# Sparse attention scores from split queries and keys, with mask and distance added on VectorE

## What is computed

```python
sc = jnp.einsum('bqgrd,bcgd->bgrqc', qb, ck).astype(f32) * scale           # compressed
sc = jnp.where(ok_c, sc - slopes[:, :, None, None] * dist_c, NEG_INF)
...
ss = jnp.where(dist_s[:, :, None] >= 0,                                     # selected
               ss - slopes[None, :, :, None, None, None] * dist_s[:, :, None], NEG_INF)
...
sw = jnp.einsum('bqgrd,bkgd->bgrqk', qb, kwb).astype(f32) * scale          # window
sw = jnp.where(ok_w, sw - slopes[:, :, None, None] * dist_w.astype(f32), NEG_INF)
p_win = jax.nn.softmax(sw, axis=-1)
...
o = gb[..., 0:1] * o_cmp + gb[..., 1:2] * o_slc + gb[..., 2:3] * o_win
```

## Time and profile before

| | |
|---|---|
| median of 3 runs | 3684.37 us (3681.41 to 3687.91) |
| span of the profiled execution | 3682.4 us |
| TensorE busy | 3545.7 us (96%) |
| VectorE busy | 1694.4 us (46%) |
| ScalarE busy | 1230.5 us (33%) |
| GpSimd busy | 204.2 us (6%) |
| `sparse_attention` | 1142.2 to 1323.3, 181.1 us |
| `compressed_and_keys` | 999.6 to 1142.2, 142.6 us |

### The profile page before, as it was taken

The page is one execution under the profiler, slowest core; times in us unless marked ns, Lnnn a source line. Parts: engine busy times, 40 slices in busy tenths (PEclk is TensorE's granted clock), DMA queues, the critical chain, the costliest instruction groups (busy, mean ns, idle before and its releaser), DMA issues. The chain is left out here.

```text
span 3682.4 us, 45186 instructions
## 1 busy us (share of the span) xinstructions
PE 3545.7 (96%) x18232; PEld 2772.9 (75%) x18232; DVE 1694.4 (46%) x2770; ACT 1230.5 (33%) x2143; POOL 204.2 (6%) x272
## 2 busy tenths in 40 slices
PE   8999999999999999999999999999999988999999
PEld 6477887888766778888878645788888846777887
DVE  6544554333404655534346524444443635655443
ACT  3223433232224653433232212311122545642222
POOL 1041201000200001000000000000000111000000
PEclk9999999999999999999999999999999989999999
DMA  4276312232210013122221201111122410012222
GB/s 175 96 284 230 124 73 77 91 115 91 107 46 24 1 58 137 47 91 100 106 91 54 79 0 46 46 69 69 49 77 80 146 40 24 1 46 72 111 92 80
DMA packets 32176, 307.90 MB, mean 84 GB/s; under 512 B 4035, under 2 KB 7844, under 8 KB 11397
## 3 DMA queue, kind: packets, MB, share of 16 engines
q1 hardware_dynamic: 32006, 305.52, 23.0%
HBM read 303.41 MB, written 2.10 MB: 83 GB/s over the span
## 5 line engine op out<-in xcount | busy, mean ns | idle before, releaser
L716 PE MATMUL psum<-operand_rounded,weights_rest 128*128 128x512 f32 (+1 forms) x1328 | 500.9, 377 | 0.4 <-DVE weights_rest L641 0.3
L717 PE MATMUL psum<-operand_rounded,weights_rounded 128*128 128x512 f32 (+1 forms) x1328 | 498.4, 375 | 0.0
L718 PE MATMUL psum<-operand_rest,weights_rounded 128*128 128x512 f32 (+1 forms) x1328 | 498.1, 375 | 0.0
L650 DVE TENSOR_TENSOR weights_rest<-ring,weights_rounded 128x1024 fp32r<-128x1024 f32 x160 | 199.8, 1248 | 399.1 <-ACT operand_rounded L611 399.1
L320 PE MATMUL psum<-operand_rounded,weights_rest 128*128 128x512 f32 (+1 forms) x1056 | 375.6, 356 | 6.3 <-DVE weights_rest L393 4.3
L321 PE MATMUL psum<-operand_rounded,weights_rounded 128*128 128x512 f32 (+1 forms) x1056 | 374.7, 355 | 0.0
L610 ACT ACTIVATE weights_rounded<-ring 128x1024 fp32r<-128x1024 f32 x160 | 169.2, 1058 | 433.8 <-PE psum L718 411.7
L716 PEld LDWEIGHTS psum<-operand_rounded,weights_rest 128*128 128x128 f32 x1328 | 250.3, 188 | 48.5 <-DVE weights_rest L641 3.2
L717 PEld LDWEIGHTS psum<-operand_rounded,weights_rounded 128*128 128x128 f32 x1328 | 250.3, 188 | 45.4 <-issue 0.5
L718 PEld LDWEIGHTS psum<-operand_rest,weights_rounded 128*128 128x128 f32 x1328 | 250.3, 188 | 45.1
L322 PE MATMUL psum<-h_rest,weights_rounded 128*128 128x512 f32 (+1 forms) x704 | 236.6, 336 | 0.0
(11 more groups left out here) (500 smaller groups left out, 6522.1 us busy)
## 6 DMA issues: line engine op xcount, KB each, us to landing
ring<-in_ff_w SPq DMA_DIRECT2D x32, 2048.0 KB, 8.1
ring<-in_w_mod SPq DMA_DIRECT2D x24, 2048.0 KB, 8.1
ring<-in_ffn_up SPq DMA_DIRECT2D x22, 2048.0 KB, 8.1
ring<-in_ffn_down SPq DMA_DIRECT2D x33, 1024.0 KB, 4.9
ring<-in_xa_wk SPq DMA_DIRECT2D x4, 2048.0 KB, 8.0
ring<-in_xa_wv SPq DMA_DIRECT2D x4, 2048.0 KB, 8.7
ring<-in_xa_wq SPq DMA_DIRECT2D x4, 2048.0 KB, 7.9
ring<-in_xa_wo SPq DMA_DIRECT2D x4, 2048.0 KB, 8.2
```

The costliest lines, as they stand in the source:

```text
L650: dve.tensor_tensor(part("weights", "rest", s, r, D), weight_rows(s, r), part("weights", "rounded", s, r, D).bitcast(F32), ALU.subtract).t ...
L716: nc.tensor.matmul(out, rest, top_in, start=first and not behind, stop=False)
L717: nc.tensor.matmul(out, top, top_in, start=False, stop=False)
L718: mm = nc.tensor.matmul(out, top, rest_in, start=False, stop=last and (not behind or m % 2 == 1))
```

## The change

In the attention loop, a head's query becomes one fp32r tile of 128 rows: the rounded query in one half of the partitions and what rounding left off in the other. The keys become two fp32r tiles, the rounded keys in both halves (K1) and their rest in both halves (K2). The scores are Qs times K1 plus Qs times K2. The 65th row and the mask product are gone. The queries are divided by the slope of their head beforehand, and VectorE reads the scores from PSUM, adds a table of distances (with -1e30 above the diagonal), scales by minus the slope, writes the result to the buffer of weights and finds its minimum, in one instruction for each branch. ScalarE's exponential then reads that buffer with scale -1, in place.

```diff
-                    pe.wait_ge(*p_ready.at(B * (u - 1)))
+                    pe.wait_ge(*s_max.at(B * (u - 1)))
                 for b in range(B):
                     base = score_bank(u, b)
-                    for cols, lhs, rhs, first, last in scores(u, b):
-                        mm = nc.tensor.matmul(k.psum[:, base + cols.start:base + cols.stop], lhs, rhs, start=first, stop=last)
-                mm.then_inc(s_ready.sem, 1)
+                    for lhs, rhs, first, last in scores(u, b):
+                        mm = nc.tensor.matmul(k.psum[:, base:base + width_of(u)], lhs, rhs, start=first, stop=last)
+                    mm.then_inc(s_ready.sem, 1)
...
-                act.wait_ge(*s_max.at(u + 1))
-                if u > lag:
-
-                    act.wait_ge(*t_ready.at(first_part[u - lag]))
                 for b in range(B):
-                    base, to = score_bank(u, b), b * BANK
-                    nc.scalar.activation(probs[:, u % (lag + 1), to:to + n], k.psum[:, base:base + n], ACT.Exp, bias=small[:, u % 4, 0, b:b + 1],
+                    act.wait_ge(*s_max.at(B * u + b + 1))
+                    part = probs[:, u % (lag + 1), b * BANK:b * BANK + n]
+                    nc.scalar.activation(part, part, ACT.Exp, scale=-1.0, bias=small[:, u % 4, 0, b:b + 1],
...
-                dve.wait_ge(*s_ready.at(u + 1))
-                nc.vector.tensor_reduce(small[:, u % 4, 0, :], score_tiles(u, n), AX_X, ALU.max, negate=True).then_inc(s_max.sem, 1)
+                away, slope = distances(u)
+                if u > lag:
+
+                    dve.wait_ge(*t_ready.at(first_part[u - lag]))
+                for b in range(B):
+                    base = score_bank(u, b)
+                    dve.wait_ge(*s_ready.at(B * u + b + 1))
+                    nc.vector.tensor_tensor_reduce(probs[:, u % (lag + 1), b * BANK:b * BANK + n], k.psum[:, base:base + n], away, -slope, 3e38,
+                                                   ALU.add, ALU.min, small[:, u % 4, 0, b:b + 1]).then_inc(s_max.sem, 1)
...
-        return [(slice(0, (t + 1) * P), Q[head, h, t * P:(t + 1) * P], rhs, True, False),
-                (slice(t * P, (t + 1) * P), mask_tiles[0], mask_tiles[1], False, True)]
+        keys, to = 4 * b + h // NSA_REP, (t + 1) * P
+        lhs = Qs[:, h, t * P:(t + 1) * P]
+        return [(lhs, K1[:, keys, 0:to], True, False), (lhs, K2[:, keys, 0:to], False, True)]
```

In `sparse_queries`, VectorE takes each result in one step of 128 partitions:

```diff
-                for half, part in enumerate((lo, hi)):
-                    op = dve.scalar_tensor_tensor(out=halves(Q[lo, 2 * n + half, :]), in0=halves(k.bank(n)[part, :]), scalar=scale,
-                                                  in1=rows[part, 2], op0=ALU.mult, op1=ALU.mult)
-                op.then_inc(taken.sem, 1)
+                dve.scalar_tensor_tensor(out=halves(q_pairs[:, n, :]), in0=halves(k.bank(n)), scalar=q_factor[:, n:n + 1],
+                                         in1=rows[:, 2], op0=ALU.mult, op1=ALU.mult).then_inc(taken.sem, 1)
```

```diff
+            for n in range(NSA_HEADS // 2):
+                cut_queries(n)
+            cut_keys(4)
+            cut_keys(5)
+            cut_compressed()
+            cut_keys(6)
             for t in range(TT):
...
                 for par in range(2):
-                    step(nc.vector.scalar_tensor_tensor(out=by_head(p)[:, par::2, :], in0=by_head(k.bank(score_bank(t, par), HN // 2)),
-                                                        scalar=1.0, in1=by_head(cmp_bias[:, t, :])[:, par::2, :],
-                                                        op0=ALU.mult, op1=ALU.add))
+                    step(nc.vector.tensor_tensor(by_head(p)[:, par::2, :], padded(k.bank(score_bank(t, par), HALF)),
+                                                 wide(slope_row)[:, par::2, :], ALU.mult))
+                for par in range(2):
+                    step(nc.vector.tensor_tensor(by_head(p)[:, par::2, :], by_head(p)[:, par::2, :],
+                                                 by_head(cmp_bias[:, t, :])[:, par::2, :], ALU.add))
                 step(nc.vector.tensor_reduce(small[:, 0, :], by_head(p), AX_X, ALU.max))
                 step(nc.vector.tensor_tensor(by_head(p), by_head(p), wide(small[:, 0, :]), ALU.subtract))
+                if t == 0:
+                    cut_keys(7)
                 dve.wait_ge(*p_exp.at(t + 1))
```

More of the change, by code:

```diff
@@ L1278, in attention, with sparse_attention @@
     o_copied.base += heads
-def sparse_attention(k, units, scores, width_of, values, compressed, gates, out, arena):
+def sparse_attention(k, units, scores, distances, width_of, values, compressed, gates, out, arena):
     nc = k.nc
@@ L2704, in pair_out @@
         return k.h[:, h // 2, t * P:(t + 1) * P]
-    sparse_attention(k, units, scores, lambda u: (units[u][0] + 1) * P, values, compressed, two_gates, pair_out, 23592)
+    sparse_attention(k, units, scores, distances, lambda u: (units[u][0] + 1) * P, values, compressed, two_gates, pair_out, 23336)
     output_product(k, norm=following, memory=True)
@@ L3028, in _ @@
         def _(pool):
-            for h in range(NSA_HEADS):
-                nc.gpsimd.memset(Q[NSA_DIM:HD, h, :], slopes[h])
+            for part in CK:
+                nc.gpsimd.memset(flat(part).bitcast(F32), 0.0).then_inc(ck_zeroed.sem, 1)
         @block.tensor
@@ L3167, in two_groups, with round_queries @@
                 m, bank = n - 4, k.bank(n % 2)
-                nc.scalar.activation(K[lo, 2 * m, :], bank[lo, :], ACT.Copy)
-                nc.scalar.activation(K[lo, 2 * m + 1, :], bank[hi, :], ACT.Copy).then_inc(taken.sem, 1)
+                for one, (own, across) in enumerate(sides):
+                    nc.scalar.activation(K1[own, 2 * m + one, :], bank[own, :], ACT.Copy).then_inc(k_rounded.sem, 1)
+                for one, (own, across) in enumerate(sides):
+                    nc.scalar.activation(K1[across, 2 * m + one, :], bank[own, :], ACT.Copy).then_inc(k_rounded.sem, 1)
+            def round_queries(n):
+                for one, (own, across) in enumerate(sides):
+                    nc.scalar.activation(Qs[own, 2 * n + one, :], q_pairs[own, n, :], ACT.Copy).then_inc(q_rounded.sem, 1)
             def by_group(n):
@@ L3188, in copy_turned @@
                     src = k.bank(6 + n % 2)[0:N_CMP, :].rearrange("p (h q) -> p h q", h=4)
-                    nc.scalar.activation(pcT[0:N_CMP, 4 * q:4 * q + 4, t * P:(t + 1) * P], src, ACT.Copy).then_inc(t_out.sem, 1)
+                    for odd in range(2):
+                        copied = nc.scalar.activation(pcT[64 * odd:64 * odd + N_CMP, 2 * q:2 * q + 2, t * P:(t + 1) * P], src[:, odd::2, :], ACT.Copy)
+                    copied.then_inc(t_out.sem, 1)
+            round_queries(0)
             for m in range(4):
                 both_shifted(m)
+                round_queries(2 * m + 1)
+                if m < 3:
+                    round_queries(2 * m + 2)
             act.wait_ge(*biased.at(4))
@@ L3202, in _ @@
             act.wait_ge(*second.at(1))
[L3203 removed]
+            act.wait_ge(*ck_zeroed.at(2))
+            for rows in (lo, hi):
+                nc.scalar.activation(CK[0][rows, :, 0:N_CMP], by_head(k.bank(4, 4 * N_CMP, lo)), ACT.Copy).then_inc(ck_rounded.sem, 1)
             two_groups(6)
             act.wait_ge(*second.at(2))
[L3206 to L3208 removed]
+            for at in (0, 64):
+                copied = nc.scalar.activation(flat(CV)[at:at + N_CMP, :], k.bank(5, 256)[0:N_CMP, :], ACT.Copy)
+            copied.then_inc(ck_copied.sem, 1)
             exponentials(0)
@@ L4444, in shape_constants @@
     c = np.arange(SEQ)
-    out["causal"] = np.where(i[None, :] > i[:, None], f(NEG), f(0)).astype(f)
-    out["key_index"] = np.broadcast_to(c.astype(f), (1, 2 * NSA_GROUPS, SEQ)).copy()
+    c = np.arange(SEQ)[None, :] - (SEQ - P)
+    out["distance"] = np.where(c > i[:, None], f(NEG), c.astype(f)).astype(f)
     end = np.arange(N_CMP) * CMP_STRIDE + CMP_LEN - 1
```

123 lines of the change are left out of this document (71 added, 52 removed).

## The result

The kernel with the change takes **3633.8 us** (median of 4 runs, 3630.8 to 3642.2) against 3685.9 us (median of 4, 3681.4 to 3687.9) for the kernel before, run beside it: 0.986 of the time before, 95% interval 0.9843 to 0.9877. The profiled execution has a span of 3631.6 us, 50.8 less than before.

The account below looks back on a forecast made before the run. TensorE was taken as the bound, with VectorE taking over at 256 and 128 keys. Loop 29.6, query product's end 2.8 and clock 3.4 made 35.8 us, rounded to 35: 3684.4 to about 3650 us, range 3636 to 3670.

Parts of the forecast that it names:

- TensorE's saving and what it leaves: Sparse loop: cheaper fp32r scores save 2.06, 1.64, 1.22, 0.46 us a pair, leaving TensorE 5.94, 4.63, 3.33, 2.41.
- level at 384: Sparse loop at 384 keys: VectorE needs 4.60 us a pair against TensorE's 4.63, so neither leads.
- the price of the minimum: VectorE's new mask instruction in the sparse loop: putting out the minimum was taken to cost 0.10 us each.
- the upper end: Highest price for the minimum: a small dependent VectorE step, about 0.19 us; forecast then 8 us worse.
- The lower end: Lowest price for the minimum: nothing, since the reduction and the sum are one pass.
- the allowance for close engines: Sparse loop: 0.15 us a pair, 4.8 us in 32 pairs, taken off because close engines miss their own sums.
- the end of the query product and its clock: Full-height VectorE steps start the next stage 2.8 us earlier; no half-clock stretch behind it gives 3.4 us more.
- part 4: Splitting queries, keys and compressed keys: extra ScalarE and VectorE work costed at nothing, up to 3 us if cover is gone.
- A: Rival: the minimum costs more than taken; 3658 us at 0.19 each, 3671 at 0.3; chance 0.14 beyond the forecast's bounds.
- B: Rival: VectorE's new instruction streams at half rate, 1.04 ns a column more; 3682 us, or 3708; chance 0.06.
- C: Rival: TensorE idles in the loop's narrow half and its clock falls to 0.5; 3687 us; chance 0.06.
- D: Rival: two fp32r products take as long as one fp32 product and its mask; 3678 us; chance 0.04.

## Why the prediction was right or wrong

**Right: TensorE's saving and what it leaves.** TensorE's own pairs were worked out as 5.94, 4.63, 3.33 and 2.41 us; 6.06, 4.74, 3.41 and 2.43 are seen where it leads (2.43 at the start of the 128-key units, until its lead is used up). The fp32r product of 128 columns at 0.11 us holds. Each sum is up to 0.12 too low, 1.9 us over the wide half.

**Right: VectorE becomes the bound in the narrow half.** The extra copy costs all of its time at 256 and 128 keys and nothing above, and the kernel with a product fewer gains nothing there. But "level at 384" was wrong: VectorE has slack there, for the next reason.

**Wrong: the price of the minimum.** "I take 0.10, as that row is the nearest in kind" is the step of the sum that failed by most. That a second instruction is there, which the prediction took as a sign for the upper end, is so; it is 0.08 us long, but it overlaps what follows. Without the minimum 0.01 us goes. With 0.01, the same sums give 3.44 and 2.66 us; 3.41 and 2.61 are measured where 3.80 and 3.02 were forecast. That is 6.3 us. The lower end, "the reduction and the sum are one pass", was the right reading, and the row on ScalarE the wrong neighbour: what counts is not how long the read-out is, but whether the next instruction may start beside it.

**Wrong: the allowance for close engines.** At 256 keys the two engines are exactly level, and the pair is as long as either (3.41). That the three units of distance between scores and transposes let each engine run on while the other catches up is my explanation; no run changes that distance. 4.8 us were taken off for nothing, beside the 1.9 us by which TensorE's sums were too low.

**Missed: the loop's start.** The forecast multiplied pairs by eight and so left the start as it was, with a stretch of 10.2 us at half clock in it (5.1 us lost) that lies in the trace of before and returns in its second execution. It is gone after. The 10.8 us that the way to the first copy got shorter are these 5.1 and the scores of six units, 0.96 us less each (2.00 us before, 1.04 after, 1155.13 to 1156.17), 5.8 together, which the forecast has among its pairs. Why the clock stays up is open. It isn't the moved wait, as its undoing shows: with it put back TensorE waits as long as before, at clock 1.00. The loop's account: 6.3 + 4.8 - 1.9 + 3.9 (the start beyond its share of pairs, less the 1.1 us at the changes of width and the end) = 13.1 us, from 29.6 to 42.7.

**Right: the end of the query product and its clock.** 2.5 us where 2.8 were forecast; the clock behind it gave 3.4. The undoing brings both back.

**Missed: the compressed scores.** That they "keep their number of weight loads", and so cost nothing and give nothing, counted matmuls and their loads and not the change between 64 and 128 rows. 16 steps at 0.30 us are 4.8.

**Missed: the longer chain behind them.** Of the 4.8 us, 2.8 are left, because the risk that part 4 named, the split of the last key tile and the softmax behind it, did come, by a longer way than the one it looked at. The first transposes are in time: the first softmax ends at 1091.68, they start at 1092.93. But in program order ScalarE copies the turned weights of a tile only after the exponentials of the next tile, and these wait for VectorE's softmax, which has two steps more in every tile (0.9 us) and for the second tile stands behind the split. ScalarE in order of time, then TensorE's waits between 1085 and 1124, both of the kernel after:

```profile
1094.94 0.62 ACT L3192 ACTIVATE arena<-arena 128x496 f32<-128x496 f32 x1 [8.13 <-DVE arena L3285]
```

```profile
PE psum L3129 <- ACT arena L3200: 1.9, 2, 1.2
```

TensorE's transposes stand twice before those copies, 0.70 us at 1096.39 and 1.22 at 1115.17, and the way to them from the group before takes 2.17 and 2.24 us instead of 1.30 and 1.16. That is 2.0 us, where the prediction had "nothing", up to 3 if the cover is gone, and took off 1. This is read from the order of time; no run undoes it.

**What carried the time out of the range.** With the minimum at nothing, no allowance and the full clock gain the prediction's own sum ends at 3638, and its range at 3636. So the two terms that were off by most, the minimum and the allowance, do not reach 3633.8 by themselves. The rest lies in two terms that stood at nothing: the half clock at the loop's start (5.1 us) and the change of rows in the compressed scores (4.8 us).

**The rivals.** A and B fell with the first rows of VectorE: next to no price for the minimum, and 0.285 us at 128 columns against 0.686 at 512, 1.04 ns a column with one source in PSUM and one in SBUF. C did not come in the kernel with the change (clock 1.00), but in the one with a second pass it did. D fell with the loop.

**Untouched layers.** The -3.4 us ahead of the last query product come and go between executions (half-clock stretches). Of the +4.0 behind the loop 2.8 do not: one later layer takes 392.2 us instead of 389.4 in the kernel after and in all its variants, and 389.4 in both executions of the kernel before. A group of 24 matmuls takes 4.20 us there instead of 4.17, with the same instructions. The cause stays open.

## What to carry to other kernels

A minimum taken in the pass that writes the data cost 0.01 us here, while the same reduction as a pass of its own cost its columns and a wait, 0.53 us a unit at 128 keys; where an engine is about to become the bound, that decides. Count what a chain of small edits does to the shape of matmuls, not only to their number: rows of 64 between rows of 128 cost on every change. Where an engine gets more steps "with time to spare", follow what else stands behind them in program order on the next engine, not only the first wait. And a forecast by repeating pieces needs a line of its own for the stretch in which they are not yet repeating, read with its clock.

## What the runs showed of the hardware that was not expected

- VectorE's read-out of an accumulator is a record of 0.08 us that costs 0.01 us start to start (0.41 us for two instructions with it, 0.39 without).
- One scalar more that is read per partition costs a VectorE instruction 0.06 us (0.26 against 0.20 us at 128 columns, for two instead of one; 0.77 against 0.71 us at 512 columns and half height, for one instead of none).
- Alternating between halves of the partitions costs VectorE the overlap: 0.77 us apart instead of 0.66.
- A change from 128 to 64 rows and back costs TensorE 0.3 us (1.75 to 2.04 us a step), about 0.2 there and 0.1 back; the matmuls of 64 rows themselves start 0.11 us apart, as those of 128 do.
- TensorE's clock was at half for 13.7 us in which it was busy throughout, and it had been busy without a gap for the 30 us ahead of the fall (compressed scores from 64 rows, busy 30.40 of 30.40 us from 1076.0 to 1106.4); it stayed at 1.00 in a stretch with 17 of 20 us busy (the kernel with a second pass, 1180 to 1200).
